# The gate panels of a block attention moved from the projection stage into the attention itself

## The reference

```python
def moba_layer(x, pos, w_in, w_out):
    h = x @ w_in                          # 1024 x 4096
    q, k, v, g = _split(h, ODD_SPLITS)    # four parts of 1024 columns
    q = rope(_heads(q, MOBA_HEADS), pos)
    k = rope(_heads(k, MOBA_HEADS), pos)
    o = moba_attention(q, k, _heads(v, MOBA_HEADS))
    return (_merge(o) * jax.nn.silu(g)) @ w_out
```

## Time and profile before

| | |
|---|---|
| three runs | 3120.51, 3126.64, 3128.22 us, median 3126.64 |
| profiled execution | span 3122.5 us; the page lists no other time of its own for it |
| PE | 3014.5 us busy, 97% of the span |
| DVE | 2007.9 us, 64% |
| ACT | 1512.8 us, 48% |
| granted clock, mean | 0.989 of full speed |
| stage in_odd, the two gate panels | 2389.25 to 2412.30 of the span |
| stage block_attention | 2413.9 to 2451.0 |
| out_odd, first real matmul | 2455.30 |

### The profile page before, as it was taken

How to read it: one execution, slowest core, us unless ns; L and a number is a source line. 1 busy time by engine, 2 the same in 40 slices (tenths; PEclk the granted TensorE clock), 3 DMA queues, 4 the chain that set the end, 5 groups by cost and what they waited for, 6 DMA issues and landing times. The chain is left out here.

```text
span 3122.5 us, 43115 instructions
## 1 busy us (share of the span) xinstructions
PE 3014.5 (97%) x17959; PEld 2637.2 (84%) x17959; DVE 2007.9 (64%) x2237; ACT 1512.8 (48%) x1692; POOL 24.1 (1%) x41
## 2 busy tenths in 40 slices
PE   7999998899999999999999999999999999999998
PEld 6889897788888899778888888998789798997898
DVE  4547647555455467498898987554555756787755
ACT  4543343334344345477777776443434445432453
POOL 0001000000000000000000000000000000000000
PEclk9999999999999999999999999999999999999999
DMA  5338650065555567599999998541445143345142
GB/s 194 132 124 265 223 185 28 9 242 189 188 189 184 173 211 243 201 361 351 354 363 350 370 349 298 174 145 60 141 167 177 42 162 135 135 152 177 55 169 95
DMA packets 197852, 606.10 MB, mean 194 GB/s; under 512 B 19648, under 2 KB 59401, under 8 KB 154394
## 3 DMA queue, kind: packets, MB, share of 16 engines
q1 hardware_dynamic: 192306, 588.23, 53.0%
q0 software_dynamic: 3872, 12.71, 1.3%
q10 hardware_dynamic: 1480, 2.41, 0.3%
HBM read 602.26 MB, written 1.05 MB: 193 GB/s over the span
## 5 line engine op out<-in xcount | busy, mean ns | idle before, releaser
L2121 DVE TENSOR_TENSOR w_lo<-ring,w_hi 128x2048 fp32r<-128x2048 f32 x336 | 769.7, 2292 | 336.2 <-ACT w_hi L2016 331.0
L2016 ACT ACTIVATE w_hi<-ring 128x2048 fp32r<-128x2048 f32 x336 | 643.1, 1915 | 367.4 <-PE ps L1963 153.4
L358 DVE TENSOR_TENSOR w_lo<-ring,w_hi 128x2048 fp32r<-128x2048 f32 (+2 forms) x209 | 469.4, 2247 | 480.1 <-ACT w_hi L349 479.4
L349 ACT ACTIVATE w_hi<-ring 128x2048 fp32r<-128x2048 f32 (+2 forms) x209 | 392.7, 1881 | 645.1 <-PE ps L470 488.4
L470 PE MATMUL ps<-h_hi,w_hi 128*128 128x256 f32 x1616 | 463.7, 287 | 17.6 <-DVE w_lo L358 10.7
L470 PE MATMUL ps<-h_lo,w_hi 128*128 128x256 f32 x1616 | 459.7, 284 | 0.0
L470 PE MATMUL ps<-h_hi,w_lo 128*128 128x256 f32 x1616 | 459.5, 284 | 0.0
L470 PEld LDWEIGHTS ps<-h_hi,w_hi 128*128 128x128 f32 x1616 | 312.5, 193 | 22.2 <-issue 17.0
L470 PEld LDWEIGHTS ps<-h_lo,w_hi 128*128 128x128 f32 x1616 | 312.6, 193 | 0.3
L470 PEld LDWEIGHTS ps<-h_hi,w_lo 128*128 128x128 f32 x1616 | 312.6, 193 | 0.0
L1926 PE MATMUL ps<-w_hi,h_hi 128*128 128x512 f32 x672 | 266.6, 397 | 1.4 <-DVE w_lo L2121 1.4
(11 more groups left out here) (539 smaller groups left out, 5544.3 us busy)
## 6 DMA issues: line engine op xcount, KB each, us to landing
ring<-in_moe_w_gate_up SPq DMA_DIRECT2D x224, 1024.0 KB, 4.9
ring<-in_moe_w_down SPq DMA_DIRECT2D x112, 1024.0 KB, 4.9
ring<-in_w_in SPq DMA_DIRECT2D x58, 1024.0 KB, 6.9
ring<-in_w_in_even SPq DMA_DIRECT2D x30, 1024.0 KB, 6.9
ring<-in_dense_w_gate_up SPq DMA_DIRECT2D x22, 1024.0 KB, 7.7
ring<-in_w_in_odd SPq DMA_DIRECT2D x16, 1024.0 KB, 6.7
arena<-in_w_ada POOLq DMA_DIRECT2D x24, 512.0 KB, 4.9
ring<-in_b_w_in SPq DMA_DIRECT2D x12, 1024.0 KB, 6.2
```

Source lines behind the costliest of these rows:

```text
L349: k.nc.scalar.activation(self.part(k.w_hi, b, m), src, ACT.Copy).then_inc(k.hi_ready, 1)
L358: k.nc.vector.tensor_tensor(self.part(k.w_lo, b, m), src, self.part(k.w_hi, b, m).bitcast(F32), ALU.subtract).then_inc(k.lo_ready, 1)
L2016: nc.scalar.activation(high(g, h), raw(g, h), ACT.Copy).then_inc(k.hi_ready, 1)
L2121: nc.vector.tensor_tensor(low(g, h), raw(g, h), high(g, h).bitcast(F32), ALU.subtract).then_inc(k.lo_ready, 1)
```

## The change

The two gate panels (g2) leave the stage in_odd and become a job of their own, marked `aside`, which is worked inside the attention. The class `Aside` holds the lists of where its parts stand: a panel's 96 matmuls are cut into eight pieces of 12 (half of the weights, one of two 128-column blocks, four of the eight row chunks), and `pieces` gives the step of each; `rounds` the step behind which ACT rounds a half panel; `rests` the two steps behind which DVE forms its `w_lo`, now in two instructions. Its results go to a fourth pair of banks, 6 and 7, so that the attention keeps two score banks instead of three. Both gate panels use this one pair, one after the other. The 18 idle turns before the first transposes go; the 8 at the end write bank 0.

The first gate panel is copied out of PSUM behind step 8 by a plain copy, without silu; ACT applies silu to it in SBUF behind step 16, and to the second panel when it copies that out behind step 17. For heads 0 to 13 ACT copies the output out of PSUM ungated (`gated`, `late`=14), and DVE multiplies by the gates in two wide products, over chunks 0 to 3 behind step 17 and 4 to 6 behind step 18. Heads 14 and 15 are gated as before.

```diff
     def place(self, r, i, j):
-        m.bank, m.before = group % SLOTS, i + group // SLOTS
+        m.bank, m.before = (SLOTS, r.asides + j) if r.aside else (group % SLOTS, i + group // SLOTS)
...
-    def rest_of_weights(self, dve, m, halves=(0, 1)):
+    def rest_of_weights(self, dve, m, halves=(0, 1), quarter=None):
...
+            if quarter is not None:
+                nk = m.r.part_shape(m.j)[0] // 2
+                at = slice(quarter * nk, (quarter + 1) * nk)
+                last = k.nc.vector.tensor_tensor(w_lo[:, at, :], src[:, at, :], w_hi[:, at, :], ALU.subtract)
+                if quarter == 1:
+                    last.then_inc(k.lo_ready, 1)
+                continue
...
-    def products(self, pe, m, by_chunk=False):
+    def products(self, pe, m, by_chunk=False, only=None):
...
+            if only and h != only[0]:
+                continue
...
+                if only and o != only[1]:
+                    continue
+                chunks = range(nk) if not only else range(only[2] * nk // 2, (only[2] + 1) * nk // 2)
...
+class Aside:
...
+        self.blocks = [(q, (h, o, half)) for q in range(len(self.panels))
+                       for h in range(2) for o in range(2) for half in range(2)]
...
+    def products(self, pe, s):
+
+        for (q, piece), at in zip(self.blocks, self.pieces):
+            if at == s:
+                self.stream.products(pe, self.place(q), only=piece)
...
+    def round(self, act, s):
+
+        for j, at in enumerate(self.rounds, 1):
+            if at == s:
+                self.half(j, lambda m, halves: self.stream.round_weights(act, m, halves))
+        for q in range(len(self.panels)):
+            if self.pieces[8 * q + 7] + 1 == s:
+                self.stream.evict(act, self.place(q), "act")
+        if s in self.act:
+            self.act[s](act)
+
+    def rest(self, dve, s):
+
+        for j, at in enumerate(self.rests, 1):
+            for quarter in range(2):
+                if at[quarter] == s:
+                    self.half(j, lambda m, halves: self.stream.rest_of_weights(dve, m, halves, quarter))
+        if s in self.dve:
+            self.dve[s](dve)
...
-def attention(k, name, groups, work, last_turns=0, scaled=True):
+def attention(k, name, groups, work, last_turns=0, scaled=True, aside=None):
...
-    score_banks = (0, 1, 6)
+    score_banks = (0, 1) if aside else (0, 1, 6)
...
-                    if s >= 3:
-                        pe.wait_ge(exp_done, s - 2)
+                    if s >= held:
+                        pe.wait_ge(exp_done, s - held + 1)
...
+                if aside:
+                    aside.products(pe, s)
                 if 2 <= s <= n_units + 1:
...
-                    if m == 0:
+                    if m == 0 and not aside:
                         turn_identity(k, 18, 7)
...
-           run("T", wo, 2048, k.h, to_tokens(v.v2), count=2),
-           run("F", wo, 3072, k.h, to_features(v.g2, func=ACT.Silu), count=2)])
+           run("T", wo, 2048, k.h, to_tokens(v.v2), count=2)])
+    s.add([run("F", wo, 3072, k.h, lambda nc, banks, p:
+               to_features(v.g2, func=ACT.Silu if p else ACT.Copy)(nc, banks, p), count=2)], aside=True)
...
+    def finish_gates(act):
+
+        beside.first_read(act)
+        k.nc.scalar.activation(v.g2[:, 0:4, :], v.g2[:, 0:4, :], ACT.Silu).then_inc(first_gates, 1)
...
+    beside = Aside(s, [0, 0, 1, 2, 4, 5, 6, 7, 9, 10, 11, 12, 13, 14, 15, 16], [-1, 3, 8, 13],
+                   [(1, 2), (4, 5), (9, 10), (14, 15)], late=14, act={16: finish_gates},
+                   dve={17: gate(0, 4, lambda dve: dve.wait_ge(first_gates, 1)),
+                        18: gate(4, 7, lambda dve: beside.all_read(dve))})
+    attention(k, "block_attention", groups, v.work2, last_turns=8, aside=beside)
```

More of the change, by code:

```diff
@@ L276, in add @@
             self.flat += [(r, p) for p in range(r.count)]
-            self.groups += r.count // r.acc if r.kind not in ("experts", "routed") else 0
+            self.asides += r.count if aside else 0
+            self.groups += r.count // r.acc if r.kind not in ("experts", "routed") and not aside else 0
             self.halves += r.count * r.parts
@@ L456, in products @@
                 closes = ends and not (r.by_rows and h == 0)
-                for c in range(nk):
+                for c in chunks:
                     if by_chunk and h in (0, r.by_rows) and o == 0:
@@ L475, in products, with evict @@
                     last = nc.tensor.matmul(out, k.ones_row[0:1, 0:P], row, start=False, stop=True)
-            if h == 0 and r.parts == 2:
+            if h == 0 and r.parts == 2 and (not only or only == (0, 1, 1)):
                 last.then_inc(k.first_half_used, 1)
-        last.then_inc(k.panel_used, 1)
+        if not only or only == (1, 1, 1):
+            last.then_inc(k.panel_used, 1)
+    def evict(self, eng, m, which):
+        k, r = self.k, m.r
+        if r.on == which and m.j % r.acc == r.acc - 1:
+            eng.wait_ge(k.panel_used, m.number + 1)
+            q = m.p if r.acc == 1 else m.j // r.acc
+            r.evict(k.nc, k.ps[:, 2 * m.bank:2 * m.bank + 2, :], q).then_inc(k.group_read[m.bank], 1)
     def stage(self, name, side=None, extra=(), source=(), features=None, norm=False, heads=None,
@@ L1219, with __init__, place, all_read @@
 WHOLE = (0, S)
+class Aside:
+    def __init__(self, stream, pieces, rounds, rests, late=0, act=None, dve=None):
+        self.stream, self.pieces, self.rounds, self.rests = stream, pieces, rounds, rests
+        self.late, self.act, self.dve = late, act or {}, dve or {}
+        self.panels = [(r, p) for r in stream.jobs[stream.at] for p in range(r.count)]
+        self.blocks = [(q, (h, o, half)) for q in range(len(self.panels))
+                       for h in range(2) for o in range(2) for half in range(2)]
+        assert len(pieces) == len(self.blocks) and all(r.parts == 2 for r, _ in self.panels)
+        assert len(rounds) == len(rests) == 2 * len(self.panels)
+    def place(self, q):
+        r, p = self.panels[q]
+        return self.stream.place(r, 0, p)
+    def all_read(self, eng):
+        m = self.place(len(self.panels) - 1)
+        eng.wait_ge(self.stream.k.group_read[m.bank], m.before + 1)
+    def first_read(self, eng):
+        m = self.place(0)
+        eng.wait_ge(self.stream.k.group_read[m.bank], m.before + 1)
+    def products(self, pe, s):
+        for (q, piece), at in zip(self.blocks, self.pieces):
+            if at == s:
+                self.stream.products(pe, self.place(q), only=piece)
+    def half(self, j, prepare):
+        if j < 2 * len(self.panels):
+            prepare(self.place(j // 2), (j % 2,))
+        else:
+            self.stream.first_of_next(prepare)
+    def round(self, act, s):
[14 more added lines that the diff above has]
+            self.dve[s](dve)
 def unit(scores, values, scale=1.0, mask=None, causal=False, n=S, factor=None, floor=False):
@@ L1253, in attention, with out_of, gated @@
     diagonals = work[:, 4:6, :].rearrange("p b (t n) -> p b t n", t=TT)
-    score_banks = (0, 1, 6)
+    score_banks = (0, 1) if aside else (0, 1, 6)
+    held = len(score_banks)
+    late = aside.late if aside else 0
+    def out_of(g):
+        _, r0, dv, _, _ = groups[g]
+        return k.ps[r0:r0 + dv, 4 + g % 2, 0:S]
+    def gated(g):
+        return groups[g][4] is not None and g >= late
     with stage(k, name) as st:
@@ L1300, in _ @@
                     if first and g >= 2:
[L1301 removed]
+                        if g - 2 < late:
+                            pe.wait_ge(k.out_copied, g - 1)
+                        else:
+                            pe.wait_ge(out_read, g - 1 - late)
                     for b, rows, first_token, to in u.blocks:
[L1303 removed]
+                        last = nc.tensor.matmul(out_of(g)[:, first_token:S], u.values(b),
                                                 exps_t[0:rows, m % 2, to:to + S - first_token],
@@ L1411, in _ @@
                     u, g, _, is_last = units[m]
-                    if is_last and groups[g][4] is None:
-                        _, r0, dv, dst, _ = groups[g]
+                    if is_last and not gated(g):
+                        dst = groups[g][3]
                         act.wait_ge(values_done, m + 1)
-                        nc.scalar.activation(dst, k.ps[r0:r0 + dv, 4 + g % 2, 0:S], ACT.Copy).then_inc(out_read, 1)
+                        nc.scalar.activation(dst, out_of(g), ACT.Copy).then_inc(k.out_copied if late else out_read, 1)
+                if aside:
+                    aside.round(act, s)
+    if aside:
+        k.stream.at += 1
 def swiglu_run(w_gate_up, w_down, experts, ff):
```

56 lines of the change are left out of this document (35 added, 21 removed).

## The result

The changed kernel takes 3136.84 us, the median of 20 runs (3129.79 to 3142.01), against 3126.64 for the kernel before, 20 runs beside it (3120.51 to 3130.85). The ratio is 1.0031, with a 95% interval from 1.0024 to 1.0037: 7.5 to 11.6 us slower, about 9.7. The forecast was +6.7 and 3133.3, in a range of 3125 to 3141.

A forecast was written before the change was run, and what follows sets the result against it. PE and DVE were taken as both close to full in the attention, only ACT having room. Terms 0.0 − 2.16 − 0.5 + 0.8 + 3.7 + 3.5 + 1.4 sum to +6.7 us, 3133.3 us, range 3125 to 3141.

The forecast's parts named there:

- Panels against pieces: in_odd loses its two gate panels (−23.05 us), the attention gains 16 pieces of 12 matmuls (+23.04): 0.0.
- Idle turns: The 18 idle identity turns on PE at the attention's start go, at 0.12 us each: −2.16 us.
- Head 14's wait: Near the attention's end a piece covers PE's 0.47 us wait for head 14's scaled probabilities: −0.5 us.
- Entries: PE's switch from fp32 score matmuls into each piece, 15 times at 0.05 us: +0.8 us.
- the filled gaps: Rival: pieces let neighbours' weights load ahead in PE's gaps, −4.5 us in place of +0.8; total 3128.0 us; chance 0.10.
- the switches both ways: Rival: each piece pays 0.18 us entering and leaving, 5.4 instead of 0.8; 3137.9 us; chance 0.22 with a second clock fall.
- The stall: PE waits before the ninth piece for ACT's copy of the first gate panel out of PSUM: +3.7 us.
- The tail: From head 14's transposes to the last gate product, ACT's chain makes 7.4 us instead of 3.93: +3.5 us.
- The clock: One 3.3 us half-clock stretch follows the ninth piece's stall: +1.4 us, between 0 and 2.8.
- The sum: All terms from in_odd's last value panel to out_odd's first real matmul: +6.7 us, giving 3133.3 us.
- What lies around the span: The 4.1 us between the profiled span of before (3122.5) and its median (3126.64), assumed to stay unchanged.
- the case "within 0.3%": Outcome called same: whole-kernel time within 9.4 us of 3126.64, about what a measurement can tell; chance 0.73.

The follow-up runs named there:

- the two delayed kernels: The kernel before with 25 or 43 more idle identity turns on PE at the block attention's end: 3132.17 us (ratio 1.0017) and 3129.69 us (1.0009).
- both copies early: Changed kernel with each gate panel copied out behind its last piece's step (7, 16) and the first panel's silu behind step 15: 3129.02 us, ratio 1.0009.

## Why the prediction was right, and what it mis-sized

- **Panels against pieces, 0.0:** right. Between the last value matmul and the first scores lie 24.88 us before (2389.04 to 2413.92) and 1.85 after; what went there came back as pieces.
- **Idle turns, −2.16:** right within 0.2. By the two delayed kernels a turn costs 0.109 (4.68/43), so 18 are 1.95. **Head 14's wait, −0.5:** it is gone (0.47).
- **Entries, +0.8:** 15 × 0.04 = +0.6. Neither the filled gaps (steps near 3.3) nor the switches both ways (3.9) happened; steps take 3.60. The Trainium skill ("Perfetto Trace Analysis", section "Optimization Strategy") says that regimes with different bottlenecks may gain from being interleaved; here both stood on PE, and the trace shows a step 0.04 above the sum of the two (2.12 + 1.44).
- **The stall, +3.7:** 3.35, from the chain that the forecast named; moving the rounding or the copy took it down by 1.80 and to nothing. The 0.35 too much is in the sum of ACT's durations: five of them made 4.6, while from 2414.40 to the copy's end at 2418.65 there are 4.25, since neighbours on ACT overlap (the copy starts 1.80 after the start of a rounding of 1.91).
- **The tail, +3.5:** 7.30 − 3.93 = +3.37. Silu starts 1.30 after the start of the table load. The drain of 1.38 us that the Trainium skill states ("ScalarE: Activation LUTs", section "What ACT_TABLE_LOAD costs") shows in no row here; by an estimate with it the tail would have been 8.8. The fall of the clock in the tail came (2450.50). It did not move DVE's last product (the tail is 7.30 without it too, with the copy ahead of the rounding), but it slowed the eight idle turns, and the stage ended 0.7 later by them: here the forecast took 0, "at most +1.4".
- **The clock, +1.4, between 0 and 2.8:** this is the term that was too small. The step failed where it put one stretch, of the length seen behind one other wait, behind the stall. In four executions with the same wait of 3.35 or 3.36 the half clock lasted 3.4, 10.2, 6.8 and 6.8 us; the mean of 6.8, at 12/29 of it, is an estimate of 2.8 lost. The row that the forecast went by was one draw of such a spread: the same wait before 1314.36 is followed by 3.4 us in the first profile of before and by 6.8 in the second. Over all runs the changed kernel has 10.6 us more at half clock, about +4. That idle time at the ninth piece brings the stretch behind it is shown: it stands in all four profiles with an idle wait of 3.35 or 3.36, and in none of the three in which the wait was taken away (early copy, both copies early) or filled (turns). That it brings all of the 10.6 is not shown; by the mean of 6.8 some 4 lie elsewhere.
- **The sum:** without its clock term the forecast is 6.7 − 1.4 = +5.3; the runs at equal clock give about 5, and the profile of after, less its two losses to the clock (1.5 and 0.7), +4.5. So the other terms were up to 0.8 too high together, and hid a part of what the clock term lacked: that is luck. With +4 for the clock that is 9.0 to 9.3, in the interval of 7.5 to 11.6. So the case "within 0.3%", given 0.73, ends on its bound of 9.4 and not in its middle: the two ratios of the same kernel are 1.0031 and 1.0025, the first a little above the bound. Above it the forecast expected the switches (0.25 for the whole); they did not come, and the clock alone led there.
- **What lies around the span:** 4.1 was taken. The execution of 3130.03 lists 3131.82, so it is 1.8; the other 2.3 are that the profiled execution of before ran that much below the median. A forecast as a difference added to the median is not touched by it.

Open is why the kernels without a stall still have more half clock than before: 78.5 (2.0) for both copies early, 80.8 (2.7) for one, and 81.4 (1.5) for 3 us of delay, but not 5. Their profiles show none of it inside the stage, so it lies elsewhere, ahead of the stage or behind it, and no run here separates where, or how much of it is chance.

## What to carry to other kernels

When matmuls are threaded into a stage whose bound is the same engine, count what the buffers' release waits for on the other engines, in their queue order: here one rounding ahead of one copy cost the stall, and two early copies and an early silu took the whole loss of the stage away. An idle wait on PE like this one of 3.35 us costs more than itself, so price the lower clock behind it as a spread of lengths, or fill the wait with work. And judge a change of less than 0.3% by many runs and their clocks, not by two profiles.

## What was not expected of the hardware

The same wait, at the same instruction, was followed by 3.4 us of half clock in one execution and by 10.2 in another, while one of 1.55 was followed by none. A delay of 2.7 us with a busy PE went with 8.5 us more at half clock per run than before had on the same chip, and one of 4.7 us with 4.3 less, which is not clear of noise; no run here shows why.
